# A sixth slot for expert weights in the room of the rotary and retention buffers

## The chip, the core and the metric

One core of a Trainium2 chip runs the whole kernel. TensorE does the matrix products and the transposes, VectorE (DVE), ScalarE (ACT) and GpSimd (POOL) the rest; SyncE (SP) only issues transfers. The metric is the device time of one execution in microseconds.

## The reference, cut to what matters

One layer of a decoder trunk on 512 tokens of width 1024, all in float32: a mixing sub-layer (sparse attention beside retention), then a channel sub-layer, a mixture of experts. What the change touches is the second:

```python
g_prob = softmax(t @ w_group + b_group);  g_top, g_sel = top_k(g_prob, 1)      # 4 groups
e_logits = (t @ w_expert + b_expert) of that group                             # 8 experts each
e_top, e_sel = top_k(softmax(e_logits), 2)
weights = g_top * e_top / sum(e_top)
for e in range(32):
    hid = silu(t @ w_gate_exp[e]) * (t @ w_up_exp[e])                          # 1024 -> 256, twice
    y = y + combine[:, e:e+1] * (hid @ w_down_exp[e])                          # 256 -> 1024
out = h_res + gate2 * rms_norm(y, g_post_ffn)
```

So 512 tokens give 1024 pairs of a token and an expert, and each of the 32 experts has 3 MiB of weights, of which every byte is needed once.

## The kernel before, in words

**Mixing stage.** Projections, rotary embedding, attention and retention run from a list of steps that `Plan` writes out by hand; each engine walks the same list. The rotary products live in `ropebuf` (2048 words of each partition), relu rows, attention transposes and the retention's inner products in `retbuf` (2560), attention masks in `score` (1152), the angles' cosines and sines in `cosT` and `sinT` (256 each), queries, keys and values in `work` (8704). Then come the output projection, the residual and the second norm, whose rows `H2` are stored to DRAM by POOL (L1693) and turned for the router.

**Routing.** `routing` on DVE turns the router's logits into the two experts of each token, counts and ranks the pairs (TensorE sums over partitions, L820 to L823), sorts the experts by count (`KEY`, `BEATS`, `PLACE`) and writes for each row of each unit which pair stands there (`pid_t`) and which token (`tok_t`). Its scratch, some thirty small tensors, lies in `retbuf` and `ropebuf`. The first two units need only the first four experts' ranks and get their rows early (`EARLY_...`, `early_tok`); the others wait for the table (`IN_ROW`, `IN_BOTH`, `late_rows`, `tok_ready`).

**Expert stage.** 32 experts are worked on in 18 units (`UNITS`), in this order: three pairs of the fixed experts 0 to 5, four pairs of less used ones, four units of one much used expert each, and seven pairs. A pair shares the 128 rows, 64 each; a single expert has all 128. `ORDER` is the experts' positions in order of use, 0 to 31, and position n has the weight slot n mod `SLOTS`. Of unit u TensorE does `turn_x` (L873: transposes of the gathered rows), `gate_up` (L883: both products into one bank), `turn_hid` (L901) and `down` (L910), in the order gate_up(u+1), turn_hid(u), turn_x(u+2), down(u). ACT and DVE gate the products, weigh the result by `row_wt` and write it to `YO`; POOL scatters it to DRAM (L1712).

**Weights.** There are five slots of 3 MiB: four in `ring`, which the mixing stage's weights used before, and the fifth over `rows` (gate and up) and the upper half of `hT` (down). `load_gate_up` (L460) issues two transfers of 1 MiB, `load_down` (L467) one, all by SP, in this order: gate and up of slots 0 and 3, the input once more, the downs of 0 and 3 after the retention, slots 1 and 2 after the output projection, slot 4 after the last row of `H2` and the last modulation. Then the refills: for unit u SP waits for gate_up(u) and loads gate and up of the positions that take its slots (`LET_IN`), and then, after down(u-1), the downs of the positions that take the slots of u-1. Names above the fixed six are read from the sorted list (`order_ready`, `value_load`).

```python
LET_IN = {u: [p for p in ORDER[SLOTS:] if UNIT_OF[ORDER[POS[p] - SLOTS]] == u] for u in range(NU)}
```

**Gathers.** POOL brings a unit's rows from DRAM into one of four buffers `XG` of 1024 words in `work`, one after another: gathers 0 and 1 after `early_tok`, 2 and 3 after `tok_ready`, and then, for each u, gather(u+4) and scatter(u). Each waits for the turning of the unit that had its buffer.

**Tail.** When all pairs are scattered, ACT reads them back, DVE adds each token's two, and the last norm and the residual follow (`combine`, `weigh`, `finish`).

Of the kernel before, what the change touches and what calls it, by code (L numbers as in the profile page):

```python
# [42 lines left out]
NOV = 2 * S // HALF  # L43
FIXED, WIDE = 6, 4
SLOTS = 5
FIRST_UNITS = 2
NEARLY = FIRST_UNITS * 2
# [4 lines left out]
NU = len(UNITS)  # L52
# [34 lines left out]
C_ID, C_CAUSAL, C_LT, C_ONES, C_FREQ, C_IOTA = 0, 128, 256, 384, 512, 576  # L87
# [146 lines left out]
def build(nc, t, out):  # L234
    plan = Plan()
    steps = plan.steps

    with ExitStack() as ctx:
        def sb(name, words, dt=F32, parts=P):
            return ctx.enter_context(nc.sbuf_tensor(name, [parts, words], dt))  # L240

        def sem(name):
            return ctx.enter_context(nc.semaphore(name))
# [5 lines left out]
        ring = sb("ring", RING * SLOT)  # L249
        xs = sb("xs", NB * D)  # L250
        hT = sb("hT", KD * S)
        work = sb("work", 4 * 2048 + 512)
        retbuf = sb("retbuf", 2560)
        ropebuf = sb("ropebuf", 2048)
        rows = sb("rows", 4 * D)
        accB, G1, S2, T2 = (rows[:, i * D:(i + 1) * D] for i in range(4))
        score = sb("score", P * (2 + 3 + 4))
        cst = sb("cst", NCONST)
        cosT = sb("cosT", NB * 64)
        sinT = sb("sinT", NB * 64)  # L260
# [12 lines left out]
        ones = cst[:, C_ONES:C_ONES + P]  # L273
# [24 lines left out]
        def gate_and_up(s):  # L298
            return ring[:, s * SLOT:s * SLOT + 2 * KD * F] if s < RING else rows[:, :]

        def down_rows(s):
            return ring[:, s * SLOT + 2 * KD * F:(s + 1) * SLOT] if s < RING else hT[:, KD * S // 2:KD * S // 2 + KF * D]

# [35 lines left out]
        unit_done, tp_done, sc_done, o_done = sem("unit_done"), sem("tp_done"), sem("sc_done"), sem("o_done")  # L339
# [18 lines left out]
        router_done = sem("router_done")  # L358
        xg_in = [sem(f"xg_in{i}") for i in range(RING)]
        gu_in = [sem(f"gu_in{i}") for i in range(SLOTS)]  # L360
# [44 lines left out]
        def bank(use):  # L405
            return ps[plan.bank[use]]
# [42 lines left out]

        XG = [work[:, (4 + i) * D:(5 + i) * D] for i in range(RING)]  # L450
        XT = [hT[:, i * KD * P:(i + 1) * KD * P].rearrange("p (k c) -> p k c", k=KD) for i in range(2)]
# [54 lines left out]
        def rt(at, n):  # L506

            return retbuf[:, at:at + NB * n].rearrange("p (b n) -> p b n", b=NB)
        LG, GMAX, GSUBV, GEXV, GSUM, GTOP = rt(0, 36), rt(144, 1), rt(152, NG), rt(168, NG), rt(184, 1), rt(188, 1)
# [5 lines left out]
        OH1, OH2, RANK = rt(704, NE), rt(832, NE), rt(960, NE)  # L515
        CNT, OV, BINC, BEX = (retbuf[:, 1088:1120], retbuf[:, 1248:1280], retbuf[:, 1280:1312], retbuf[:, 1312:1344])
        MFL, TMP = rt(1120, NE), rt(1600, NE)
        KEY, PLACE, ROOM, FIRST = (retbuf[:, 1472 + i * NE:1472 + (i + 1) * NE] for i in range(4))
        LATE, BIG, SHIFT, ORDV, EXC = (retbuf[:, 2288 + i * NE:2288 + (i + 1) * NE] for i in range(5))
        TILE, ROW = (retbuf[:, at:at + 2 * NB].rearrange("p (b j) -> p b j", b=NB) for at in (1728, 1736))  # L520
        WHERE = retbuf[:, 1744:1744 + 2 * NB].rearrange("p (b j) -> p b j", b=NB)
        OVC = retbuf[:, 1760:1760 + NOV * NE].rearrange("p (o e) -> p o e", o=NOV)
        EO = retbuf[:, 2448:2448 + NOV]
        BEATS = ropebuf[:, 0:NE * NE].rearrange("p (e f) -> p e f", e=NE)

        IN_ROW = ropebuf[:, 0:2 * NB * P].rearrange("p (n c) -> p n c", n=2 * NB)
        IN_BOTH = ropebuf[:, 1024:1024 + 4 * NB * NT].rearrange("p (n w t) -> p n w t", n=2 * NB, w=2)
        IN_TILE, IN_WT = IN_BOTH[:, :, 0, :], IN_BOTH[:, :, 1, :]
        row_wt = retbuf[:, 1408:1408 + NT]

        CUM = retbuf[:, 1344:1472].rearrange("p (b n) -> p b n", b=NB)
        BOTH = retbuf[:, 704:960].rearrange("p (j b e) -> p j b e", j=2, b=NB)
        RANK_AT, EARLY_AT = rt(2464, NEARLY), rt(2480, NEARLY)
        EARLY_MUL = retbuf[:, 2496:2528].rearrange("p (j b e) -> p j b e", j=2, b=NB)
        EARLY_POS, SECOND, EARLY_ROW = (retbuf[:, 2528 + i * 2 * NB:2536 + i * 2 * NB] for i in range(3))
        EARLY_PAIR = retbuf[:, 228:244].rearrange("p (t n) -> p t n", t=2)
        EARLY_IN = ropebuf[:, 1024:2048].rearrange("p (n c) -> p n c", n=2 * NB)
        SORTED, WHOLE = (retbuf[:, 1344 + i * NE:1376 + i * NE] for i in range(2))


        @block.sync
        def _(sp):
# [31 lines left out]
            for e in (0, 3):  # L574
                load_down(sp, e, e, down_in[e])
            for e in (1, 2):
                sp.wait_ge(*used_up(LAST_IN[e]))
                load_gate_up(sp, e, e, gu_in[e])
                load_down(sp, e, e, down_in[e])
            sp.wait_ge(h2_ready, NB)  # L580
            sp.wait_ge(mod_done, 8)
            load_gate_up(sp, RING, RING, gu_in[RING])
            load_down(sp, RING, RING, down_in[RING])
            named = {p: p for p in range(FIXED)}
            for u in range(NU + 1):
# [26 lines left out]
        def _(pe):  # L612
# [149 lines left out]
            def project():  # L762
# [56 lines left out]
                o = take(pe, ("rank",))  # L819
                pe.matmul(o[:, 0:NB * NE], cst[:, C_LT:C_LT + P], retbuf[:, 256:384], start=True, stop=False)  # L820
                pe.wait_ge(oh_ready, 2)
                pe.matmul(o[:, NE:NB * NE], ones, retbuf[:, 1344:1344 + (NB - 1) * NE], start=False, stop=True)
                pe.matmul(o[:, NB * NE:(NB + 1) * NE], ones, CUM[:, NB - 1, :], start=True,  # L823
# [46 lines left out]
            def turn_x(u):  # L870
                pe.wait_ge(xg_in[u % RING], 16 * (u // RING + 1))
                for q in range(2):
                    if u >= 1:  # L873
                        pe.wait_ge(xt_ev, 2 * u - 1 + q)
                    v = XG[u % RING].rearrange("p (q k) -> p k q", k=KD)
                    for c in range(4):
                        mm = pe.transpose(ps[XT_BANK[q]][:, c * P:(c + 1) * P], v[:, 4 * q + c, :], ident)
                    mm.then_inc(xt_mm, 1)
# [286 lines left out]
        def _(dve):  # L1165
# [136 lines left out]
            def routing():  # L1302
# [4 lines left out]
                def flat(x):  # L1307
                    return x.rearrange("p b n -> p (b n)")
# [7 lines left out]

                prod = retbuf[:, 384:512].rearrange("p (b e g) -> p b e g", b=NB, e=EPG)
                for b in range(NB):
                    last = v.tensor_tensor(prod[:, b, :, :], LG[:, b, NG:].rearrange("p (g e) -> p e g", g=NG),
                                           SG[:, b, :].unsqueeze(1).to_broadcast([P, EPG, NG]), ALU.mult)  # L1320
                link(last)
                link(v.tensor_reduce(flat(EL), retbuf[:, 384:512].rearrange("p (q g) -> p q g", g=NG), AX, ALU.add))
                first_best(EL, EMAX, ET, EM, numbers(EPG), EPG, O1)
# [18 lines left out]
                dve.wait_ge(rank_done, 1)  # L1342
                link(v.tensor_copy(retbuf[:, 960:1120], bank(("rank",))[:, 0:(NB + 1) * NE]))
                link(v.tensor_tensor(RANK_AT, RANK[:, :, 0:NEARLY],
# [313 lines left out]
        def _(pool):  # L1658
# [41 lines left out]
            def gather(u):  # L1700

                if u >= RING:
                    pool.wait_ge(xt_mm, 2 * (u - RING) + 2)
                    pool.wait_ge(xg_in[u % RING], 16 * (u // RING))
                g.indirect_dma_start(out=XG[u % RING], out_offset=None, in_=h2_dram,
                                     in_offset=bass.IndirectOffsetOnAxis(ap=tok_t[:, u:u + 1], axis=0),
                                     bounds_check=token_bound, oob_is_err=False).then_inc(xg_in[u % RING], 16)

# [6 lines left out]

            for u in range(RING):
                if u == FIRST_UNITS:
                    pool.wait_ge(tok_ready, 1)
                gather(u)
            for u in range(NU):  # L1720
                if u + RING < NU:
                    gather(u + RING)
                scatter(u)
# [47 lines left out]
```

## Time and profile before

| | |
|---|---|
| median of 3 runs | 743.2 us (742.86 to 745.53) |
| the profiled execution | 741.91 us |
| its span | 739.8 us |
| TensorE, matmuls | 647.3 us busy (88% of the span) |
| TensorE, weight loads | 320.5 us (43%) |
| DVE | 373.4 us (50%) |
| ACT | 159.8 us (22%) |
| POOL | 79.4 us (11%) |
| DMA | 171.76 MB, mean 232 GB/s |
| granted TensorE clock, mean | 0.966 |

The span runs from the first to the last instruction; the execution's own time has 2.1 us more around it. Busy shares are averages over stages with different limits, so the page's 40 slices and the table of stages say more than this one. A busy TensorE is not TensorE at its peak: matmuls are pipelined and their ends are modelled. Idle time of an engine is put down to what ended it, and to "issue" where nothing that the profile follows did, as with a wait for a transfer of SP's queue.

### The profile page before, as it was taken

What the parts mean: (1) busy time and instruction counts of PE and PEld (TensorE: products, weight loads), DVE (VectorE), ACT (ScalarE), POOL (GpSimd) and SP (SyncE); (2) the same over time, 40 slices, a digit from 0 to 9 for tenths busy, and PEclk for the clock granted to TensorE, in tenths of its full rate; (3) what the DMA queues carried; (4) which work ended last, traced back from release to release, by engine and by line L of the source; (5) the groups of instructions that cost most, each with busy time, mean ns of one, the idle gap of its engine ahead of it and who ended that gap; (6) DMA issues with size and microseconds to landing.
All of it is one profiled execution on the core that took longest, in us unless ns stands there. A gap on an engine that the chain in (4) does not pass through costs nothing. (4 is left out here: it accounts for less than half of the span.)

```text
span 739.8 us, 7183 instructions
## 1 busy us (share of the span) xinstructions
PE 647.3 (88%) x2514; PEld 320.5 (43%) x2514; DVE 373.4 (50%) x722; ACT 159.8 (22%) x334; POOL 79.4 (11%) x105
## 2 busy tenths in 40 slices
PE   1699999999999999999999988999788999878730
PEld 1455544444455555556644554433233544333210
DVE  5764266989776763247933258623112233212218
ACT  1420021133122223310222231112111212111113
POOL 0013221210111110000000001121111221200010
PEclk9999999999999999999999999999989999999975
DMA  9991706150606060250641085799999999999426
GB/s 327 389 346 64 277 3 226 23 205 5 224 0 228 2 223 5 106 156 3 262 193 57 29 353 204 292 418 420 422 420 421 421 410 394 420 419 412 163 77 270
DMA packets 50132, 171.76 MB, mean 232 GB/s; under 512 B 10032, under 2 KB 10032, under 8 KB 37168
## 3 DMA queue, kind: packets, MB, share of 16 engines
q1 hardware_dynamic: 41824, 154.98, 53.9%
q0 software_dynamic: 5888, 10.52, 3.8%
q10 hardware_dynamic: 2384, 5.80, 2.1%
q8 instruction: 21, 0.34, 0.2%
q14 instruction: 15, 0.12, 0.0%
HBM read 168.13 MB, written 13.63 MB: 246 GB/s over the span
## 5 line engine op out<-in xcount | busy, mean ns | idle before, releaser
L623 PE MATMUL psum<-ring,hT 128*128 128x512 f32 (+1 forms) x576 | 234.8, 561 | 0.0
L623 PEld LDWEIGHTS psum<-ring,hT 128*128 128x128 f32 x576 | 102.7, 191 | 119.3 <-issue 119.0
L897 PE MATMUL psum<-ring,hT 128*64 128x512 f32 (+1 forms) x416 | 127.8, 635 | 19.5 <-issue 19.5
L897 PEld LDWEIGHTS psum<-ring,hT 128*64 128x64 f32 (+1 forms) x416 | 43.6, 152 | 90.8 <-issue 90.6
L1593 DVE TENSOR_SCALAR work<-work 128x256 f32<-128x256 f32 x18 | 5.3, 294 | 141.2 <-PE psum L907 114.4
L923 PE MATMUL psum<-ring,work 128*64 128x512 f32 (+1 forms) x208 | 63.4, 613 | 5.1 <-issue 3.6
L774 PE MATMUL psum<-ring,hT 128*128 128x512 f32 x128 | 55.8, 594 | 1.6 <-ACT work L1060 0.9
L1207 DVE SCALAR_TENSOR_TENSOR rows<-ring,sm,rows 128x512 f32<-128x512 f32 x64 | 51.1, 799 | 1.7
L897 PE MATMUL psum<-rows,hT 128*64 128x512 f32 (+1 forms) x96 | 42.4, 595 | 1.8 <-issue 1.8
L1105 ACT ACTIVATE work<-psum 128x256 f32<-128x256 f32 x18 | 6.9, 383 | 171.0 <-PE psum L897 171.0
L1268 DVE TENSOR_TENSOR ropebuf<-psum,cosT 128x512 f32<-128x512 f32 (+1 forms) x24 | 14.7, 614 | 51.4 <-PE psum L623 39.1
L1712 POOL DMA_INDIRECT pair_rows<-work,pid_t x18 | 18.0, 1000 | 204.8 <-DVE work L1605 204.8
L1675 POOL TENSOR_TENSOR ropebuf<-ropebuf 128x256 f32<-128x256 f32 (+1 forms) x28 | 18.8, 673 | 180.0 <-DVE ropebuf L1268 180.0
L774 PEld LDWEIGHTS psum<-ring,hT 128*128 128x128 f32 x128 | 24.0, 190 | 30.7 <-issue 29.7
L923 PEld LDWEIGHTS psum<-ring,work 128*64 128x64 f32 (+1 forms) x208 | 20.1, 147 | 31.8 <-issue 30.9
L998 ACT ACTIVATE work<-psum 128x512 f32<-128x512 f32 (+1 forms) x24 | 12.6, 542 | 90.3 <-PE psum L635 85.0
L1595 DVE RECIPROCAL work<-work 128x256 f32<-128x256 f32 x18 | 31.5, 1753 | 0.6
L1605 DVE TENSOR_SCALAR work<-psum,retbuf 128x512 f32<-128x512 f32 x18 | 13.5, 751 | 33.4 <-PE psum L923 33.4
L645 PE MATMUL psum<-cst,work 128*64 128x1 f32 x64 | 8.3, 259 | 23.1 <-DVE work L1207 23.1
L1280 DVE MAX8 sm<-score 128x8 f32<-128x256 f32 (+2 forms) x48 | 26.9, 560 | 1.4
L1489 DVE CUSTOM_DVE_ANT_0 xs<-psum,score 128x256 f32<-128x256 f32 (+2 forms) x24 | 12.4, 555 | 29.4 <-PE psum L727 29.4
L1281 DVE MATCH_REPLACE8 score<-sm,score 128x256 f32<-128x256 f32 (+2 forms) x48 | 26.0, 542 | 0.0
(245 smaller groups left out, 737.7 us busy)
## 6 DMA issues: line engine op xcount, KB each, us to landing
ring<-in_w_gate_exp SPq DMA_DIRECT2D x26, 1024.0 KB, 13.7
ring<-in_w_up_exp SPq DMA_DIRECT2D x26, 1024.0 KB, 21.4
ring<-in_w_down_exp SPq DMA_DIRECT2D x26, 1024.0 KB, 23.1
ring<-in_w_in SPq DMA_DIRECT2D x8, 2048.0 KB, 10.0
ring<-in_w_ada SPq DMA_DIRECT2D x8, 2048.0 KB, 14.9
ring<-in_w_ada SPq DMA_DIRECT2D x7, 1024.0 KB, 13.1
rows<-in_w_gate_exp SPq DMA_DIRECT2D x6, 1024.0 KB, 14.0
rows<-in_w_up_exp SPq DMA_DIRECT2D x6, 1024.0 KB, 22.3
```

Source lines behind the costliest of these rows:

```text
L623: mm = pe.matmul(o[:, 0:width], hT3[:, k, b * P:(b + 1) * P], w[:, k, :], start=(k == 0), stop=(k == KD - 1))
L774: mm = pe.matmul(o[:, :], hT3[:, k, b * P:(b + 1) * P], w[:, k, :], start=(k == 0), stop=(k == KD - 1))
L897: mm = pe.matmul(o[rows, :], XT[u % 2][:, k, rows], both(SLOT_OF[place])[:, k, :, :], start=(k == 0), stop=(k == KD - 1))
L923: mm = pe.matmul(o[rows, :], HT[u % 2][:, i, rows], down_of(SLOT_OF[place])[:, i, n * 512:(n + 1) * 512], start=(i == 0), stop=(i == KF - 1))
L1207: ins = v.scalar_tensor_tensor(out=acc, in0=w[:, k, :], scalar=sc_[:, k:k + 1], in1=acc, op0=ALU.mult, op1=ALU.add)
L1268: ins = v.tensor_tensor(dst, src, tb, ALU.mult)
L1280: link(v.max(top8, m))
L1281: link(v.match_replace(m, top8, m, TAKEN))
L1595: v.reciprocal(e, e).then_inc(gu_step, 1)
L1605: v.tensor_scalar(YO[u % 2][:, 512:1024], ps[Y_BANK[(2 * u + 1) % 3]][:, :], row_wt[:, u:u + 1], None, ALU.mult).then_inc(y_evV, 1)
L1675: g.tensor_tensor(dst[:, :, 0, :], xc[:, :, 0, :], xs_[:, :, 1, :], ALU.subtract)
L1712: g.indirect_dma_start(out=y_dram, out_offset=bass.IndirectOffsetOnAxis(ap=pid_t[:, u:u + 1], axis=0), in_=YO[u % 2], in_offset=None, boun ...
```

## The change

The number of slots goes from 5 to 6. The new slot's gate and up lie over `ropebuf` and the first 2048 words of `retbuf`, which become one tensor, `both_bufs`; its down lies over words 6144 to 8191 of `work`, where `H2[1]`, an ACT scratch and the gather buffers 2 and 3 were. The gathers keep two buffers. What the routing kept in the two old buffers goes to `score`, `cosT`, `sinT`, the lower 2048 words of `work` and the last 512 words of `retbuf`. The order of the refills follows from `SLOTS`. POOL issues gathers 0, 1 and 2 at the start and then, for each u, gather(u+3) and scatter(u).

```diff
-SLOTS = 5
+SLOTS = 6
+GATHERS = 2
...
-        retbuf = sb("retbuf", 2560)
-        ropebuf = sb("ropebuf", 2048)
+        both_bufs = sb("both_bufs", 2048 + 2560)
+        ropebuf, retbuf = both_bufs[:, 0:2048], both_bufs[:, 2048:4608]
...
         def gate_and_up(s):
-            return ring[:, s * SLOT:s * SLOT + 2 * KD * F] if s < RING else rows[:, :]
+            if s < RING:
+                return ring[:, s * SLOT:s * SLOT + 2 * KD * F]
+            return rows[:, :] if s == RING else both_bufs[:, 0:2 * KD * F]
 
         def down_rows(s):
-            return ring[:, s * SLOT + 2 * KD * F:(s + 1) * SLOT] if s < RING else hT[:, KD * S // 2:KD * S // 2 + KF * D]
+            if s < RING:
+                return ring[:, s * SLOT + 2 * KD * F:(s + 1) * SLOT]
+            return hT[:, KD * S // 2:KD * S // 2 + KF * D] if s == RING else work[:, 6 * D:8 * D]
...
-        xg_in = [sem(f"xg_in{i}") for i in range(RING)]
+        xg_in = [sem(f"xg_in{i}") for i in range(GATHERS)]
...
-        XG = [work[:, (4 + i) * D:(5 + i) * D] for i in range(RING)]
+        XG = [work[:, (4 + i) * D:(5 + i) * D] for i in range(GATHERS)]
...
-            return retbuf[:, at:at + NB * n].rearrange("p (b n) -> p b n", b=NB)
+            return score[:, at:at + NB * n].rearrange("p (b n) -> p b n", b=NB)
...
-        BEATS = ropebuf[:, 0:NE * NE].rearrange("p (e f) -> p e f", e=NE)
-
-        IN_ROW = ropebuf[:, 0:2 * NB * P].rearrange("p (n c) -> p n c", n=2 * NB)
+        BEATS = work[:, 0:NE * NE].rearrange("p (e f) -> p e f", e=NE)
+
+        IN_ROW = work[:, 0:2 * NB * P].rearrange("p (n c) -> p n c", n=2 * NB)
...
@@ SP @@
             for e in (0, 3):
                 load_down(sp, e, e, down_in[e])
+            sp.wait_ge(ret_ss, RHEADS)
+            load_gate_up(sp, RING + 1, RING + 1, gu_in[RING + 1])
             for e in (1, 2):
...
             load_down(sp, RING, RING, down_in[RING])
+            sp.wait_ge(h2_out[1], 16 * (NB // 2))
+            sp.wait_ge(res_sq, NB)
+            sp.wait_ge(tp_done, plan.tp[("h2", NB - 1, 1)] + 1)
+            load_down(sp, RING + 1, RING + 1, down_in[RING + 1])
...
@@ TensorE @@
-                pe.wait_ge(xg_in[u % RING], 16 * (u // RING + 1))
+                pe.wait_ge(xg_in[u % GATHERS], 16 * (u // GATHERS + 1))
...
@@ POOL @@
-                if u >= RING:
-                    pool.wait_ge(xt_mm, 2 * (u - RING) + 2)
-                    pool.wait_ge(xg_in[u % RING], 16 * (u // RING))
+                if u >= GATHERS:
+                    pool.wait_ge(xt_mm, 2 * (u - GATHERS) + 2)
+                    pool.wait_ge(xg_in[u % GATHERS], 16 * (u // GATHERS))
...
-            for u in range(RING):
+            for u in range(GATHERS + 1):
                 if u == FIRST_UNITS:
                     pool.wait_ge(tok_ready, 1)
                 gather(u)
             for u in range(NU):
-                if u + RING < NU:
-                    gather(u + RING)
+                if u + GATHERS + 1 < NU:
+                    gather(u + GATHERS + 1)
                 scatter(u)
```

## Rows read from the trace of the kernel before

**Rows 1.** The page, 40 slices of 18.5 us: TensorE and DMA busy tenths, transfer rate.

```profile
PE   1699999999999999999999988999788999878730
...
DMA  9991706150606060250641085799999999999426
GB/s 327 389 346 64 277 3 226 23 205 5 224 0 228 2 223 5 106 156 3 262 193 57 29 353 204 292 418 420 422 420 421 421 410 394 420 419 412 163 77 270
```

**Rows 2.** Stage table: us, engines' busy us, last three: granted clock, DMA share, GB/s.

```profile
452.80:466.50 13.70, 12.41 (x57) 5.30 (x56) 12.16 (x56) 2.18 (x5) 2.09 (x2) 1.00 0.09 24
522.40:574.40 52.00, 44.49 (x165) 17.98 (x166) 10.94 (x15) 7.78 (x15) 5.04 (x5) 0.88 1.02 421
574.40:621.70 47.30, 47.30 (x166) 21.72 (x166) 14.59 (x20) 10.19 (x20) 9.07 (x9) 1.00 0.99 407
666.40:691.90 25.50, 20.19 (x102) 8.30 (x99) 7.29 (x10) 5.26 (x10) 1.98 (x2) 1.00 0.91 373
```

**Rows 3.** Instructions in order of time, TensorE: start, us, line; bracket: idle before.

```profile
456.80 1.16 PE L877 MATMUL psum<-cst,work 128*128 128x128 f32 x8 [0.95 <-DMA work<-h_rows,tok_t]
...
459.36 7.09 PE L897 MATMUL psum<-ring,hT 128*64 128x512 f32 x32
...
522.37 8.43 PE L897 MATMUL psum<-ring,hT 128*64 128x512 f32 x32 [5.11 <-issue]
...
605.97 0.64 PE L897 MATMUL psum<-ring,hT 128*64 128x512 f32 x1
...
613.33 1.06 PE L877 MATMUL psum<-cst,work 128*128 128x128 f32 x8
...
617.75 7.09 PE L897 MATMUL psum<-ring,hT 128*64 128x512 f32 x32
...
691.87 8.78 PE L897 MATMUL psum<-ring,hT 128*64 128x512 f32 x32 [3.45 <-issue]
...
706.53 3.65 PE L923 MATMUL psum<-ring,work 128*64 128x512 f32 x16 [0.68 <-ACT work L1111]
```

**Rows 4.** Issues of SP's queue in order of time: start, us that the issue took.

```profile
372.51 0.81 SPq L469 DMA_DIRECT2D ring<-in_w_down_exp  x2
...
466.49 0.33 SPq L464 DMA_DIRECT2D ring<-in_w_gate_exp  x1
...
652.07 0.33 SPq L464 DMA_DIRECT2D rows<-in_w_gate_exp  x1
...
670.23 0.38 SPq L465 DMA_DIRECT2D ring<-in_w_up_exp  x1
...
675.02 13.77 SPq L469 DMA_DIRECT2D ring<-in_w_down_exp  x2
```

**Rows 5.** Issue to landing of the last up half, issued at 670.23 (L465).

```profile
DMA to landing us min/median/max: 21.5/21.5/21.5
```

**Rows 6.** DMA queues, 675 to 695 us in 40 parts of 0.5 us: rate.

```profile
GB/s 442 426 442 410 393 426 426 442 426 410 434 352 443 377 475 336 402 311 344 279 295 295 279 229 246 197 229 229 197 213 262 377 426 459 393 238 107 131 98 98
```

**Rows 7.** Issue to landing of the last down half, issued at 688.5 (L469).

```profile
DMA to landing us min/median/max: 11.4/11.4/11.4
```

**Rows 8.** Issue to landing of the first refill's gate half, 466.49 (L464).

```profile
DMA to landing us min/median/max: 4.9/4.9/4.9
```

**Rows 9.** Instructions in order of time, POOL: store of h2, gathers (L1705).

```profile
435.09 0.53 POOL L1693 DMA_DIRECT2D h_rows<-work  x1 [15.87 <-DVE work L1581]
453.47 1.07 POOL L1705 DMA_INDIRECT work<-h_rows,tok_t  x1 [17.86 <-issue]
...
597.50 1.01 POOL L1705 DMA_INDIRECT work<-h_rows,tok_t  x1 [0.30 <-issue]
```

**Rows 10.** Issue to landing of h2's last store, issued at 435.09 (L1693).

```profile
DMA to landing us min/median/max: 8.6/8.6/8.6
```

**Rows 11.** Issue to landing of slot 4's first down, issued at 435.66 (L469).

```profile
DMA to landing us min/median/max: 17.0/17.0/17.0
```

**Rows 12.** Issue to landing of all 18 gathers (L1705).

```profile
DMA to landing us min/median/max: 3.3/10.1/12.7
```

More of the change, by code:

```diff
@@ L506, in rt, with spare @@
         def rt(at, n):
-            return retbuf[:, at:at + NB * n].rearrange("p (b n) -> p b n", b=NB)
+            return score[:, at:at + NB * n].rearrange("p (b n) -> p b n", b=NB)
+        def spare(at, n):
+            return retbuf[:, 2048 + at:2048 + at + n]
         LG, GMAX, GSUBV, GEXV, GSUM, GTOP = rt(0, 36), rt(144, 1), rt(152, NG), rt(168, NG), rt(184, 1), rt(188, 1)
@@ L515, in build @@
         OH1, OH2, RANK = rt(704, NE), rt(832, NE), rt(960, NE)
[L516 to L520, printed above, removed]
@@ L521, in build @@
-        WHERE = retbuf[:, 1744:1744 + 2 * NB].rearrange("p (b j) -> p b j", b=NB)
-        OVC = retbuf[:, 1760:1760 + NOV * NE].rearrange("p (o e) -> p o e", o=NOV)
-        EO = retbuf[:, 2448:2448 + NOV]
-        BEATS = ropebuf[:, 0:NE * NE].rearrange("p (e f) -> p e f", e=NE)
-        IN_ROW = ropebuf[:, 0:2 * NB * P].rearrange("p (n c) -> p n c", n=2 * NB)
-        IN_BOTH = ropebuf[:, 1024:1024 + 4 * NB * NT].rearrange("p (n w t) -> p n w t", n=2 * NB, w=2)
-        IN_TILE, IN_WT = IN_BOTH[:, :, 0, :], IN_BOTH[:, :, 1, :]
@@ L529, in build @@
[L529 to L536, printed above, removed]
@@ L537, in build @@
-        EARLY_IN = ropebuf[:, 1024:2048].rearrange("p (n c) -> p n c", n=2 * NB)
-        SORTED, WHOLE = (retbuf[:, 1344 + i * NE:1376 + i * NE] for i in range(2))
+        CNT = score[:, 1088:1120]
+        MFL, TMP = (cosT[:, i * P:(i + 1) * P].rearrange("p (b n) -> p b n", b=NB) for i in range(2))
+        KEY, PLACE, ROOM, FIRST = (sinT[:, i * NE:(i + 1) * NE] for i in range(4))
+        LATE, BIG, SHIFT, ORDV, EXC, OV, BINC, BEX = (spare(i * NE, NE) for i in range(8))
+        TILE, ROW, WHERE = (spare(256 + i * 2 * NB, 2 * NB).rearrange("p (b j) -> p b j", b=NB) for i in range(3))
@@ new lines, in build @@
+        EARLY_POS, SECOND, EARLY_ROW = (spare(280 + i * 2 * NB, 2 * NB) for i in range(3))
+        EO = spare(304, NOV)
+        OVC = score[:, 384:384 + NOV * NE].rearrange("p (o e) -> p o e", o=NOV)
+        BEATS = work[:, 0:NE * NE].rearrange("p (e f) -> p e f", e=NE)
+        IN_ROW = work[:, 0:2 * NB * P].rearrange("p (n c) -> p n c", n=2 * NB)
+        IN_BOTH = work[:, 1024:1024 + 4 * NB * NT].rearrange("p (n w t) -> p n w t", n=2 * NB, w=2)
+        IN_TILE, IN_WT = IN_BOTH[:, :, 0, :], IN_BOTH[:, :, 1, :]
@@ new lines, in build @@
+        row_wt = sinT[:, 192:192 + NT]
+        CUM = sinT[:, 128:256].rearrange("p (b n) -> p b n", b=NB)
+        BOTH = score[:, 704:960].rearrange("p (j b e) -> p j b e", j=2, b=NB)
+        RANK_AT, EARLY_AT = (spare(at, NB * NEARLY).rearrange("p (b n) -> p b n", b=NB) for at in (320, 336))
+        EARLY_MUL = spare(352, 2 * NB * NEARLY).rearrange("p (j b e) -> p j b e", j=2, b=NB)
+        EARLY_PAIR = score[:, 228:244].rearrange("p (t n) -> p t n", t=2)
+        EARLY_IN = work[:, 1024:2048].rearrange("p (n c) -> p n c", n=2 * NB)
@@ L541, in _ @@
+        SORTED, WHOLE = (sinT[:, 128 + i * NE:128 + (i + 1) * NE] for i in range(2))
         @block.sync
@@ L819, in project @@
                 o = take(pe, ("rank",))
-                pe.matmul(o[:, 0:NB * NE], cst[:, C_LT:C_LT + P], retbuf[:, 256:384], start=True, stop=False)
+                pe.matmul(o[:, 0:NB * NE], cst[:, C_LT:C_LT + P], score[:, 256:384], start=True, stop=False)
                 pe.wait_ge(oh_ready, 2)
-                pe.matmul(o[:, NE:NB * NE], ones, retbuf[:, 1344:1344 + (NB - 1) * NE], start=False, stop=True)
+                pe.matmul(o[:, NE:NB * NE], ones, sinT[:, 128:128 + (NB - 1) * NE], start=False, stop=True)
                 pe.matmul(o[:, NB * NE:(NB + 1) * NE], ones, CUM[:, NB - 1, :], start=True,
@@ L874, in turn_x @@
                         pe.wait_ge(xt_ev, 2 * u - 1 + q)
-                    v = XG[u % RING].rearrange("p (q k) -> p k q", k=KD)
+                    v = XG[u % GATHERS].rearrange("p (q k) -> p k q", k=KD)
                     for c in range(4):
@@ L1315, in routing @@
                 v.tensor_tensor(GSUBV, LG[:, :, 0:NG], GMAX.to_broadcast([P, NB, NG]), ALU.subtract).then_inc(g_sub, 1)
-                prod = retbuf[:, 384:512].rearrange("p (b e g) -> p b e g", b=NB, e=EPG)
+                prod = score[:, 384:512].rearrange("p (b e g) -> p b e g", b=NB, e=EPG)
                 for b in range(NB):
@@ L1321, in routing @@
                 link(last)
-                link(v.tensor_reduce(flat(EL), retbuf[:, 384:512].rearrange("p (q g) -> p q g", g=NG), AX, ALU.add))
+                link(v.tensor_reduce(flat(EL), score[:, 384:512].rearrange("p (q g) -> p q g", g=NG), AX, ALU.add))
                 first_best(EL, EMAX, ET, EM, numbers(EPG), EPG, O1)
@@ L1342, in routing @@
                 dve.wait_ge(rank_done, 1)
-                link(v.tensor_copy(retbuf[:, 960:1120], bank(("rank",))[:, 0:(NB + 1) * NE]))
+                link(v.tensor_copy(score[:, 960:1120], bank(("rank",))[:, 0:(NB + 1) * NE]))
                 link(v.tensor_tensor(RANK_AT, RANK[:, :, 0:NEARLY],
@@ L1700, in gather @@
             def gather(u):
-                if u >= RING:
-                    pool.wait_ge(xt_mm, 2 * (u - RING) + 2)
-                    pool.wait_ge(xg_in[u % RING], 16 * (u // RING))
-                g.indirect_dma_start(out=XG[u % RING], out_offset=None, in_=h2_dram,
+                if u >= GATHERS:
+                    pool.wait_ge(xt_mm, 2 * (u - GATHERS) + 2)
+                    pool.wait_ge(xg_in[u % GATHERS], 16 * (u // GATHERS))
+                g.indirect_dma_start(out=XG[u % GATHERS], out_offset=None, in_=h2_dram,
                                      in_offset=bass.IndirectOffsetOnAxis(ap=tok_t[:, u:u + 1], axis=0),
-                                     bounds_check=token_bound, oob_is_err=False).then_inc(xg_in[u % RING], 16)
+                                     bounds_check=token_bound, oob_is_err=False).then_inc(xg_in[u % GATHERS], 16)
             def scatter(u):
```

## The prediction

> **What bounds the kernel now.** I read the 40 slices first. Up to about 460 us TensorE is the full engine and the DMA engines come and go; from 481 to 684 us the DMA share is 9 tenths or more in every slice and the rate stands at 394 to 422 GB/s [rows 1]. That is the expert stage: 32 experts of three 1 MiB transfers (gate, up, down; 1.049 MB each). The stage table agrees: share 1.02 and 0.99, 421 and 407 GB/s [rows 2]. TensorE looks busy there too, but its own rows show that it waits: gate_up(5) starts at 522.37 after an idle of 5.11 us and gate_up(17) at 691.87 after 3.45 us, both put down to "issue", that is, to nothing that the program's engines did [rows 3]. For the last one the landing can be matched: the up half of the last expert, issued at 670.23, landed 21.5 us later, at 691.7 [rows 4, 5]. So the stage ends when the weights have come, and then 18.3 us of TensorE (to 710.2, the end of down(17)) and 29.6 us of scatter, read-back and output follow.
>
> TensorE's own pace is faster. From gate_up(11) to gate_up(12) it needs 617.75 - 605.97 = 11.8 us without a wait [rows 3]. From gate_up(0) at 459.36, 17 steps of 11.8 us would start gate_up(17) at 660, not 691.9. TensorE therefore has about 32 us of room before it becomes the bound.
>
> **Where the stream of weights starts and what it carries.** The DMA engines are nearly idle from 452.8 to 466.5 us (share 0.09) [rows 2]: all five slots are full, and the next load waits for gate_up(0). It is issued at 466.49 [rows 4]. From there to the landing at 691.7, which are counted in transfers: with five slots 27 experts are still to come, 81 transfers, of which three (the downs of the experts at positions 29, 30 and 31 in order of use) are issued behind the last up: 78. So one transfer costs 225.2 / 78 = 2.89 us, gathers and scatters included. By the mean rate of 421 GB/s it would be 1.049 / 0.421 = 2.49 us. The two differ because a transfer ends when its last DMA engine ends. From 675 to 695 us the rate sinks from 442 to 197 GB/s while the last up is still on its way [rows 6]: most engines are through, some lag. The last down alone, issued at 688.5 into engines that were by then mostly free, took 11.4 us, the first one of the stream, at 466.49, took 4.9 [rows 7, 8].
>
> I take **2.8 us**, near the counted price, since the lagging engines are the ones that end the last up, and keep 2.49 and 2.89 as the ends. The Trainium skill (DMA: Bandwidth & Descriptors, Where 436 GB/s comes from) says that between HBM and SBUF a core's HBM share of about 358 GB/s is what binds; the trace shows 421, so that figure does not hold here. By it a transfer would cost an estimated 2.9 us and four of them 11.7.
>
> **The change, part by part.**
>
> 1. *Sixth slot, count.* 26 experts instead of 27 have to come after gate_up(0): three transfers fewer in the stream.
>
> 2. *Sixth slot, order at the end.* With five slots position 31 reuses the slot of position 26 and is asked for after gate_up(15). With six, positions 30 and 31 follow 24 and 25, both after gate_up(14), where SP now asks for 29 and 30 (the block that starts at 652.07 [rows 4]). The downs of 28 to 31 all stand behind the last up: 78 - 74 = 4 transfers fewer ahead of it, three from point 1 and one from the order. The gain at gate_up(17) is 4 x 2.8 = **11.2 us** (10.0 to 11.6); if the order gave nothing, 3 x 2.49 = 7.5.
>
> 3. *Is the last down in time?* It lands at 688.5 + 11.4 = 699.9 now [rows 7], and three transfers earlier, at about 691.5, after. down(17) would start at 706.53 - 11.2 = 695.3: 3.8 us of cover. If it is gone, its excess is lost one for one.
>
> 4. *Loading the sixth slot.* The gate and up halves are issued behind the downs of slots 0 and 3 (372.51 [rows 4]) and the wait in front of them, for the retention's sums, has ended by then, since the wait before it needs those sums. 2.1 MB go into three slices, 370 to 425 us, with 193, 57 and 29 GB/s [rows 1]: 5 us of DMA, cost nothing. Behind them on SP stand the loads of slots 1 and 2, which wait for the output projection and start after those slices, so SP loses two issues in an idle time. Without that cover the price would be 5 us.
>
> 5. *The down half of the sixth slot.* It waits for the last store of h2: issued at 435.09, landed after 8.6 us, so at 443.7 [rows 9, 10]. Then it queues behind slot 4, whose down was issued at 435.7 and landed 17.0 us later, at 452.7 [rows 11], and ends at about 455.2. The first gather is issued at 453.47 and TensorE waited 0.95 us for it at 456.80 [rows 9, 3]. It now runs beside the end of that load. Nothing to 2.5 us; I take **+0.5 us**, since most of the transfer lies ahead of the gather. The wait on SP costs nothing: the refill behind it is due at 466.49.
>
> 6. *The refill.* The first two are now positions 6 and 7, and both names come from the sorted list on SP; reading the first stands ahead of the wait for gate_up(0). No cost.
>
> 7. *Two gather buffers.* After scatter(u-1) POOL issues gather(u+3) instead of gather(u+4). In the tightest stretch the issue is at 597.50, and as it would be gather(12), it is due at turn_x(12), 613.33 [rows 9, 3]: 15.8 us, against 10.1 median and 12.7 longest [rows 12]. The wait for the turning of unit u+1 has ended by then, and scatter(u) behind it is not held up. Cost nothing, with 3.1 us of cover; beyond, each excess delays a unit.
>
> 8. *The routing's scratch.* Same instructions and shapes, other addresses, no new wait; BEATS and IN_ROW lie in rooms that the same engine has finished with, and YO is written after the table. No cost; I put 0.5 us either way in the range.
>
> Sum: -11.2 + 0.5 = -10.7 us. The profiled execution took 741.9 us (span 739.8); the median of the runs is 743.2, 1.3 above. So 731.2 for such an execution and **732.5 us** for the median. TensorE stays off the bound: gate_up(17) at 681, against the 660 that it could reach.
>
> **Rivals.**
>
> *A. Only the count helps (12%).* If the lagging engines do not set the end, or the order gives nothing, 3 x 2.49 = 7.5 us less 1 to 3 of points 5 and 3: 737 to 739. For it: the mean rate is nearly flat; against: the matched landing.
>
> *B. The slots also starved the stream (14%).* The share is 0.99 and 407 GB/s in the stretch of single experts and 0.91 and 373 at the end [rows 2]. Full rate would give back 47.3 x 14/421 = 1.6 us and 25.5 x 48/421 = 2.9 us: -15.2, or 728.
>
> *C. The gathers become the bound (slower, 4%).* With two buffers a gather that lands more than 15.8 us after its issue stops TensorE in every unit. The loop then runs over two units, so an excess counts once in two. To be slower by 3.7 us gate_up(17) must start at 695.6, 35.6 us behind TensorE's own 660; over the 14 units from the fourth on, seven loops, that is 5.1 us each, a landing time of 20.9 us. At 22 us it is 7 x 6.2 = 43 us, gate_up(17) at 703.4, 11.5 later than now: 755. Against it: the landing time does not follow the depth of the weight queue. Its longest was 12.7 us, while the last up took 21.5 from issue to landing [rows 12, 5]. The Trainium skill (DMA: Bandwidth & Descriptors, Queues, rings and completion order) has each DMA engine go round between its queues packet by packet, so a longer weight queue would not push a gather back; the trace agrees.
>
> *D. No difference (7%).* The stream itself gets slower, because it is deeper. With 74 transfers a price of 3.03 us instead of 2.89 gives the whole gain back: 743, between 740 and 746. For it: the counted price is above the mean already, so the DMA engines are not evenly loaded; against: the rate was level from 481 to 592 us [rows 1]. TensorE's clock decides nothing here: it was granted 0.88 from 522.4 to 574.4, where TensorE waited for weights, and 1.00 behind that [rows 2], and gate_up took 8.43 us rather than 7.09 [rows 3], but such a loss lies inside time that the weights set. At the last unit (8.78 us) it is in the 18.3 us already.
>
> The main case keeps 63%. Its own range is 730 to 735. A gain below 0.5% (3.7 us) could not be told from none. The range reaches to B at the lower end and to A at the upper: 727.5 to 738.5. Faster by over 0.5%: main, A and B, 0.89; same 0.07; slower 0.04.
>
> **What would show it.** Right: no wait before gate_up(5); gate_up(17) starts near 681, still after a wait, with the last up landing just before; DMA share near 1 up to about 680; 29.6 us after down(17) as before; gathers land in 10 to 13 us and no turn_x from the third on waits for one. Point 2 is wrong if the gain at gate_up(17) is near 7.5 while three transfers fewer are gone; point 5 if gate_up(0) starts after 460.4. The whole is wrong if gate_up(17) starts without a wait for weights, or if TensorE waits for gathers in the middle of the stage.

## The result and the profile after

| | before | after |
|---|---|---|
| median | 743.03 us (4 runs, 741.62 to 745.53) | 730.72 us (4 runs, 730.48 to 731.33) |
| ratio | | 0.9833, interval 0.9812 to 0.9853 |
| profiled execution, its span | 741.91 us, 739.8 us | 730.83 us, 728.6 us |

12.3 us less by the medians, 11.1 by the profiled executions. The forecast was 732.5 us with a range of 727.5 to 738.5. A second set of runs of the same kernel (e5 below) had 733.9 us beside 743.9 for the kernel before, 10.0 us less: the forecast lies between the two sets.

The page's slices of the kernel after, for [rows 1]:

```profile
PE   1599999999999999999999989999997999788830
...
PEclk9999999999999999999999999999998999999975
DMA  9991806060705042070391059399999999999526
GB/s 327 391 359 34 299 15 231 0 231 0 232 0 197 34 130 103 2 237 29 130 396 81 30 233 400 127 415 421 421 418 423 420 419 421 420 417 413 220 89 264
```

The rate now stands between 413 and 423 GB/s from the 27th slice to the 37th; the dip to 394 of the 34th slice before (610 to 629 us, right behind the units of single experts) is gone. A table of stages shows the stretch of those units (last three columns: granted clock, DMA share, GB/s), and how the last gate_up was clocked:

```profile
570.00:620.00 50.00, 48.41 (x181) 21.54 (x179) 16.05 (x23) 11.07 (x21) 8.07 (x8) 1.00 1.02 420
682.70:689.70 7.00, 7.00 (x33) 2.59 (x33) 0.00 (x0) 0.00 (x0) 0.80 (x1) 1.00 0.38 155
```

TensorE in order of time, for [rows 3]; the bracket is the idle time ahead:

```profile
457.49 1.16 PE L892 MATMUL psum<-cst,work 128*128 128x128 f32 x8 [1.16 <-DMA work<-h_rows,tok_t]
...
460.04 7.09 PE L912 MATMUL psum<-ring,hT 128*64 128x512 f32 x32
...
607.02 1.51 PE L912 MATMUL psum<-ring,hT 128*64 128x512 f32 x6 [0.61 <-issue]
...
682.66 7.09 PE L912 MATMUL psum<-ring,hT 128*64 128x512 f32 x32 [1.74 <-issue]
...
695.62 3.65 PE L938 MATMUL psum<-ring,work 128*64 128x512 f32 x16 [0.68 <-ACT work L1126]
```

gate_up(0) starts at 460.04, gate_up(17) at 682.66, 222.6 us later. Before it was 691.87 - 459.36 = 232.5 [rows 3]. **That distance is the measure of all that follows**, since it leaves out how the mixing stage went. The difference is 9.9 us. gate_up(5) no longer waits; the first wait for weights comes in unit 6, ahead of down(6). Behind gate_up(17) stand 16.6 us to the end of down(17) at 699.27, against 18.3 before, and 29.3 against 29.6 to the end of the span. So the span's 11.2 us are 9.9 at the last weights, 1.7 in the last gate_up (7.09 against 8.78 us), 0.3 in the tail, less 0.7 by which gate_up(0) starts later.

SP's issues, for [rows 4]: the down of the sixth slot, the first refill, the last up half, the last two downs.

```profile
444.37 0.33 SPq L474 DMA_DIRECT2D work<-in_w_down_exp  x1
467.33 0.36 SPq L469 DMA_DIRECT2D ring<-in_w_gate_exp  x1
...
654.98 2.14 SPq L470 DMA_DIRECT2D ring<-in_w_up_exp  x1
...
663.62 5.35 SPq L474 DMA_DIRECT2D ring<-in_w_down_exp  x2
```

From issue to landing, of the last up half (L470):

```profile
DMA to landing us min/median/max: 27.6/27.6/27.6
```

It landed at 682.6, and gate_up(17) started at 682.66: the stage still ends with the weights. The gathers (L1720), for [rows 12]:

```profile
DMA to landing us min/median/max: 3.5/10.2/11.9
```

### The profile page after: what moved, and what is told of

It reads as the page before. It is cut to its first block and busy times, and to the rows that moved or that the text cites. A ratio compares the mean times of both kernels' runs of the same rounds, so it can differ in the third digit from the quotient of the medians.

```text
span 728.6 us, 7186 instructions
## 1 busy us (share of the span) xinstructions
PE 644.6 (88%) x2514; PEld 319.8 (44%) x2514; DVE 373.5 (51%) x722; ACT 159.8 (22%) x334; POOL 79.5 (11%) x105
## 5 line engine op out<-in xcount | busy, mean ns | idle before, releaser
L912 PE MATMUL psum<-ring,hT 128*64 128x512 f32 (+1 forms) x352 | 85.0, 594 | 4.4 <-issue 4.4
L912 PEld LDWEIGHTS psum<-ring,hT 128*64 128x64 f32 (+1 forms) x352 | 30.0, 142 | 57.2 <-issue 56.2
L938 PE MATMUL psum<-ring,work 128*64 128x512 f32 (+1 forms) x176 | 46.5, 632 | 4.7 <-issue 4.1
L912 PE MATMUL psum<-rows,hT 128*64 128x512 f32 (+1 forms) x80 | 38.6, 639 | 8.4 <-issue 8.4
L1283 DVE TENSOR_TENSOR both_bufs<-psum,cosT 128x512 f32<-128x512 f32 (+1 forms) x24 | 14.7, 614 | 51.4 <-PE psum L638 39.1
L912 PE MATMUL psum<-both_bufs,hT 128*64 128x512 f32 (+1 forms) x80 | 38.6, 640 | 0.0
L1690 POOL TENSOR_TENSOR both_bufs<-both_bufs 128x256 f32<-128x256 f32 (+1 forms) x28 | 18.8, 673 | 180.4 <-DVE both_bufs L1283 180.4
L1013 ACT ACTIVATE work<-psum 128x512 f32<-128x512 f32 (+1 forms) x24 | 12.6, 542 | 90.3 <-PE psum L650 85.0
L1620 DVE TENSOR_SCALAR work<-psum,sinT 128x512 f32<-128x512 f32 x18 | 13.5, 751 | 34.9 <-PE psum L938 34.9
L912 PEld LDWEIGHTS psum<-rows,hT 128*64 128x64 f32 (+1 forms) x80 | 12.4, 157 | 32.6 <-issue 32.6
```

The source lines that it names most:

```text
L912: mm = pe.matmul(o[rows, :], XT[u % 2][:, k, rows], both(SLOT_OF[place])[:, k, :, :], start=(k == 0), stop=(k == KD - 1))
L938: mm = pe.matmul(o[rows, :], HT[u % 2][:, i, rows], down_of(SLOT_OF[place])[:, i, n * 512:(n + 1) * 512], start=(i == 0), stop=(i == KF - 1))
L1013: a.activation(dst, src, ACT.Copy).then_inc(evac, 1)
L1283: ins = v.tensor_tensor(dst, src, tb, ALU.mult)
L1620: v.tensor_scalar(YO[u % 2][:, 512:1024], ps[Y_BANK[(2 * u + 1) % 3]][:, :], row_wt[:, u:u + 1], None, ALU.mult).then_inc(y_evV, 1)
L1690: g.tensor_tensor(dst[:, :, 0, :], xc[:, :, 0, :], xs_[:, :, 1, :], ALU.subtract)
```

## The experiments

Nine more kernels ran and the changed one once more (e5), each timed beside the kernel before on the same chip; the ratio is to that one, whose median was 743.1 to 743.9 us in these sets. In the table "distance" is that from gate_up(0) to gate_up(17), in the profiled execution.

| kernel | median, us | ratio to before (interval) | distance, us | last gate_up, us |
|---|---|---|---|---|
| before | 743.0 | | 232.5 | 8.78 |
| after | 730.7 | 0.983 (0.981 to 0.985) | 222.6 | 7.09 |
| e1 | 740.8 | 0.996 (0.993 to 0.999) | 230.1 | 8.78 |
| e2 | 743.8 | 1.000 (0.998 to 1.001) | 232.5 | 8.69 |
| e3 | 739.0 | 0.993 (0.991 to 0.994) | 227.9 | 9.19 |
| e4 | 732.6 | 0.984 (0.982 to 0.986) | 221.0 | 7.09 |
| e5 (after again) | 733.9 | 0.986 (0.982 to 0.989) | 222.5 | 8.78 |
| e6 | 727.3 | 0.978 (0.975 to 0.980) | 218.4 | 7.09 |
| e7 | 730.0 | 0.981 (0.979 to 0.984) | 216.7 | 8.74 |
| e8 | 731.5 | 0.983 (0.980 to 0.987) | 221.4 | 7.09 |
| e9 | 731.0 | 0.982 (0.978 to 0.986) | 221.3 | 7.09 |
| e10 | 737.4 | 0.991 (0.988 to 0.995) | 228.3 | 8.78 |

### e1: the sixth slot filled late

```diff
-            sp.wait_ge(ret_ss, RHEADS)
-            load_gate_up(sp, RING + 1, RING + 1, gu_in[RING + 1])
...
+            sp.wait_ge(gu_mm, 1)
+            load_gate_up(sp, RING + 1, RING + 1, gu_in[RING + 1])
             load_down(sp, RING + 1, RING + 1, down_in[RING + 1])
```

> The changed kernel with six slots, but the sixth slot's three transfers are asked for only after gate_up(0), at the head of the refills. Theory (the gain is the number of transfers that stand between gate_up(0) and the last up half, 2.9 us each): 77 of them stand there instead of 74 in the changed kernel and 78 in the one before, so gate_up(17) starts about 8.7 us later than in the changed kernel and the time is 739 to 741 us. Rival (six slots help because the stream is starved less with five, whenever the sixth is filled): most of the gain stays, 731 to 734 us.

740.8 us, as the theory expected (739 to 741); gate_up(0) and gate_up(17):

```profile
461.73 7.09 PE L912 MATMUL psum<-ring,hT 128*64 128x512 f32 x32
...
691.79 8.78 PE L912 MATMUL psum<-ring,hT 128*64 128x512 f32 x32 [2.09 <-issue]
```

The theory holds: six slots without the early fill keep only 2.4 of the 9.9 us. The price is smaller than expected, though: 7.5 us for three transfers, 2.5 each and not 2.9.

### e2: two gather buffers and five slots

The edit is that of the change to `XG`, `xg_in`, `gather` and the two loops that call it, on the kernel before.

> The kernel before with five slots and two gather buffers instead of four, nothing else. Theory (a gather lands within 13 us and has 15.8): no difference, 742 to 744 us, and no turning of rows waits for a gather from unit 3 on. Rival (the second half of the buffers was worth something and the changed kernel pays for it): slower by 1 us or more, with waits for gathers in the stretch of single experts.

743.8 us, distance 232.5. What TensorE waited for from 470 to 700 us (us in total, times, longest):

```profile
PE psum L898 <- issue: 19.7, 7, 3.8
PE psum L924 <- issue: 6.3, 2, 5.5
PE psum L878 <- DMA work<-h_rows,tok_t: 1.4, 1, 1.4
```

One wait for a gather, the one of unit 2 behind the table, which the kernels before and after have too. The two buffers cost nothing.

### e3: the last expert's gate and up behind two downs

```diff
+            held = []
             for u in range(NU + 1):
                 for place in LET_IN.get(u, []):
+                    if place == ORDER[-1]:
+                        named[place] = ...
+                        held.append(place)
+                        continue
...
                     load_down(sp, named[place], SLOT_OF[place], down_in[SLOT_OF[place]])
+                if held:
+                    place = held.pop()
+                    load_gate_up(sp, named[place], SLOT_OF[place], gu_in[SLOT_OF[place]])
```

> The changed kernel, but gate and up of the last expert (position 31) are issued behind the downs of positions 28 and 29 instead of ahead of them: 76 transfers instead of 74 up to the last up half. Theory (each transfer ahead of the last up costs 2.5 to 2.9 us at the end, whichever it is): 735.7 to 736.5 us, gate_up(17) later by 5 to 6 us. Rival (only the number of experts that come after gate_up(0) counts, the order at the end gives nothing): 730 to 731.5 us.

739.0 us, more than either expected. gate_up(0) and gate_up(17):

```profile
460.85 7.09 PE L921 MATMUL psum<-ring,hT 128*64 128x512 f32 x32
...
688.72 9.19 PE L921 MATMUL psum<-ring,hT 128*64 128x512 f32 x32 [7.03 <-issue]
```

The distance grew by 5.3 us, 2.6 for each of the two transfers: the order at the end counts as much as the number. SP's issue of the last up half came at 660.19 instead of 654.98 us and its landing 6.0 us later: with the order the issue moved as well. The rest of the 8.3 us between the profiled spans (736.9 and 728.6) is the clock of the last gate_up, 2.1 us longer behind a wait of 7.03 us, and a start 0.8 us later.

### e4 and e5: the first refill in halves, and the changed kernel again

```diff
+            for piece in range(PIECES):
+                sp.wait_ge(*((gu_piece, piece + 1) if piece < PIECES - 1 else (gu_mm, 1)))
+                for place in LET_IN[0]:
+                    slot, w = SLOT_OF[place], KD * F
+                    at, lo, hi = gate_and_up(slot), piece * w // PIECES, (piece + 1) * w // PIECES
+                    sp.dma_start(at[:, lo:hi], pick(wg_d, named[place])[:, lo:hi]).then_inc(gu_in[slot], 16)
+                    sp.dma_start(at[:, w + lo:w + hi], pick(wu_d, named[place])[:, lo:hi]).then_inc(gu_in[slot], 16)
...
+                    if u == 0 and k < KD - 1 and (k + 1) % (KD // PIECES) == 0:
+                        mm.then_inc(gu_piece, 1)
```

> The changed kernel, but gate and up of the first two refills (positions 6 and 7) are loaded in two halves each: the halves that gate_up(0) has read by its middle are asked for there, 3.5 us before its end. Theory (the stream of weights is the bound from its first transfer to its last up half, so what starts it earlier ends it earlier): 3 to 3.5 us less, 727 to 728 us. Rival (the start of the stream does not set its end, since somewhere between the engines wait for free slots): 730 to 731.5 us.

> The changed kernel as it is, as the level for the two kernels beside it. From gate_up(0) to gate_up(17) it should need 222 to 223 us as in its first profile, and 730 to 732 us in all. If the halved first refill had really cost time in the run before (732.6 us), this one must come out below it by over 1 us relative to the kernel before; if that was the start of the run alone, the two are equal in relation to it.

732.6 us, where the changed kernel had 730.7 in one set of runs and 733.9 in another. gate_up(0) and (17) of e4, then of e5:

```profile
464.10 7.09 PE L925 MATMUL psum<-ring,hT 128*64 128x512 f32 x32
...
685.12 7.09 PE L925 MATMUL psum<-ring,hT 128*64 128x512 f32 x32 [1.76 <-issue]
```

```profile
463.33 7.09 PE L912 MATMUL psum<-ring,hT 128*64 128x512 f32 x32
...
685.86 8.78 PE L912 MATMUL psum<-ring,hT 128*64 128x512 f32 x32 [2.08 <-issue]
```

The distance of e5 is 222.5 us, as in the first profile, but its gate_up(0) came at 463.33 and its last gate_up took 8.78 us: the same code is 5.1 us longer in this execution (733.7 against 728.6), all of it outside the distance. Of the 3.3 us by which gate_up(0) came later, 2.5 arose between the last store of `H2` (435.55 and 436.06) and the first gather (453.96 and 457.00), and there TensorE's clock did it. Here are the router's last-but-one products (L811), the modulation's (L700) and the stretch from 432 to 436 us (third number from the right: granted clock), first in the changed kernel and then in e5:

```profile
430.16 1.98 PE L811 MATMUL psum<-work 128*128 128x36 f32 x16 [0.79 <-ACT work L1013]
431.97 1.96 PE L700 MATMUL psum<-rows,cst 128*128 128x512 f32 x4
...
432.00:436.00 4.00, 3.48 (x14) 1.70 (x14) 3.42 (x5) 0.44 (x3) 0.45 (x1) 1.00 1.01 420
```

```profile
430.67 3.51 PE L811 MATMUL psum<-work 128*128 128x36 f32 x16 [0.79 <-ACT work L1013]
433.99 3.76 PE L700 MATMUL psum<-rows,cst 128*128 128x512 f32 x4
...
432.00:436.00 4.00, 4.00 (x14) 2.97 (x14) 2.67 (x3) 0.95 (x3) 0.00 (x0) 0.50 1.01 426
```

From that store to the first gather it is 20.9 us in e4, e5, e6 and e7, 19.3 in e1 and 18.4 in all others. The changed kernel itself had a granted clock of 0.50 from 440 to 442 us, where only TensorE's filling products were running and it cost nothing. The three traces with five slots have no such loss there; the same code has it or not (e5 and the changed kernel), so whether six slots make it more frequent is open. By the distance, which leaves this out, the halves are a gain of 1.5 us, not the 3.5 by which their stream starts earlier, and nothing that the medians show; e5's own median, 733.9, lies above the 730 to 732 that it was expected to have. So neither the theory nor its rival holds as put: something under half arrives. Where the rest goes was not settled.

### e6, e7 and e10: the rows of a unit spread over the partitions

```diff
+    c[:, C_SPREAD + r // HALF * HALF + r % HALF // 32 * 32 + r % 8 * 4 + r // 8 % 4] = r + 1
...
-                v.tensor_tensor(IN_ROW, in_pairs(ROW, P), iota(P), ALU.is_equal)
+                v.tensor_tensor(IN_ROW, in_pairs(ROW, P), cst[:, C_SPREAD:C_SPREAD + P].unsqueeze(1).to_broadcast(
+                    [P, 2 * NB, P]), ALU.is_equal)
```

`EARLY_IN` compares with the same constants, and the row numbers start at 1.

> The changed kernel, but the rows of a unit lie in another order within each half of 64 partitions: row r at partition 32*(r/32) + 4*(r mod 8) + (r/8 mod 4), so that 8 neighbouring rows lie 4 partitions apart. Gathers and scatters leave empty rows out, and the full ones stand at the start of each half, so the DMA engines that serve those partitions move more. Theory (this load is what makes some DMA engines lag, and the lag, not the mean rate, ends the last up half): the lag of up to 20 us between first and last engine of one transfer shrinks, gate_up(17) comes 6 to 9 us earlier and the time is 722 to 725 us. Rival (certain DMA engines are slow whatever rows they move): 730 to 732 us and the rate sinks before the last landing as before.

> The spread rows together with the first refill in halves (asked for 3.5 us earlier). Theory (one stream from its start to its last landing, and without the lag nothing else holds it up): 2.5 to 3.5 us less than with the spread rows alone. Rival (the earlier start is lost again within the stage): less than 1 us of difference to the spread rows alone.

> The kernel before, five slots and four gather buffers, with the spread rows alone. Theory (a part of its 232.5 us from gate_up(0) to gate_up(17) is the lag of the DMA engines that move the full rows, the same with five slots as with six, and no part of the price of a transfer): 3.5 to 4.5 us less there, 738 to 740 us. Rival (the lag builds up only with the deeper queue of six slots, or the spread rows help by something else): no difference to the kernel before, 742 to 744 us.

e6: 727.3 us, the fastest of the study; its interval lies wholly below that of e5, timed beside it. Expected were 722 to 725 us and 6 to 9 us in the stage, so the theory has the direction and too large a size. gate_up(0) and (17) of e6:

```profile
463.00 7.09 PE L915 MATMUL psum<-ring,hT 128*64 128x512 f32 x32
...
681.42 7.09 PE L915 MATMUL psum<-ring,hT 128*64 128x512 f32 x32 [1.71 <-issue]
```

The distance fell by 4.1 us. How the lag went shows in the rate, in 40 parts of 0.625 us. The changed kernel, 660 to 685 us:

```profile
GB/s 420 420 419 419 419 393 419 433 419 419 419 419 419 419 406 374 446 400 393 420 393 380 367 380 367 393 341 354 301 301 301 288 288 288 288 249 236 236 236 203
```

The same stretch with the rows spread:

```profile
GB/s 407 419 419 406 419 433 419 419 419 419 419 419 419 439 406 439 393 407 406 433 433 433 419 419 419 419 433 406 433 433 419 406 393 380 341 315 354 308 236 210
```

In the first the rate is below 400 GB/s for nearly all of the last 12 us, in the second for the last 5: the DMA engines finish closer together. (gate_up(17) starts at 682.66 us in the first and at 681.42 in the second.) The traces hold the same more directly, in the times of a transfer's sixteen semaphore increments, taken here for the ends of sixteen engines' shares: those of the last down half run from 673.2 to 693.1 us in the changed kernel, 19.9 us, and from 680.2 to 691.7 in e6, 11.5 us. With five slots, for the down half of position 30, it is 14.3 us in the kernel before and 8.9 in e10. Nothing but the rows' places differs, so how the rows lie sets a good part of the lag. That the full rows side by side at the start of each half load some engines more is the reading that the order was made for; no view shows which engines they are.

The Trainium skill (DMA: Bandwidth & Descriptors, The descriptor swizzle) says for a transfer over 128 partitions which of them one engine serves, four neighbours and the four that lie 32 above. The order of e6 was made after it, and the run agrees in so far as spreading by it helped; the section does not speak of gathers of single rows. The Trainium skill (DMA: Bandwidth & Descriptors, Latency and other measured facts) names two engines as usually slower than the others. No run here shows that, but something of the kind may be what is left: the rate still sinks at the end.

The same edit on the kernel before (e10) gave 737.4 us and a distance of 228.3, 4.2 less. The lag is there with five slots as with six and has no share in the change. With the halves as well (e7) the distance is 1.7 us shorter still, nearly as between e5 and e4 (1.5), but the last gate_up took 8.74 us instead of 7.09 and the median is 2.7 us above that of e6. Neither side of its expectation came: the theory wanted 2.5 to 3.5 us less, the rival under 1 us of difference. The median's loss is not explained by the two traces, whose spans are 727.6 and 727.3 us; e6's is that of its slowest execution.

### e8 and e9: dummy products ahead of the last gate_up

e8 is e6 with this edit, e9 is e7 with it.

```diff
+                if u == NU - 1:
+                    pe.wait_ge(xt_ev, 2 * NU)
+                    stream(ps[XT_BANK[0]], 4)
```

> The changed kernel with spread rows, and before gate_up(17) TensorE runs four dummy products into a free bank (1.7 us) where it used to wait for the last weights. Theory (the longer last gate_up, 8.8 instead of 7.1 us in some executions, comes from the idle wait ahead of it): gate_up(17) takes 7.1 us, its start is not later, and the median is 0 to 1.7 us below the spread rows alone (726 to 727.5 us). Rival (the clock answers to the longer waits of the units before, or to nothing that TensorE does here): 8.8 us again in about half of the executions, the time as with the spread rows alone.

> Spread rows, the first refill in halves and the dummy products together. From gate_up(0) to gate_up(17) 216.7 us as with the first two; with the last gate_up at 7.1 instead of 8.7 us the time is 724 to 726 us if the theory of the clock holds, 727 to 730 us if it does not.

A miss, by a size: the four products of e8 took 3.70 us, not 1.7.

```profile
679.35 3.70 PE L778 MATMUL psum<-cst 128*128 128x512 f32 x8
682.98 7.09 PE L918 MATMUL psum<-ring,hT 128*64 128x512 f32 x32
```

gate_up(17) ran at 7.09 us in both, but 3 us (e8) and 4.6 us (e9) later than without them by the distance, and the medians, 731.5 and 731.0, are above those of e6 and e7 and above all that was expected of either. The theory of the clock is neither shown nor refuted by them: the wait and the clock were changed with a delay that hides the gain. It stands on the other rows: after waits of 1.71 to 1.76 us the last gate_up took 7.09 us (after, e4, e6), after waits of 2.08 to 3.47 it took 8.69 to 8.78 (before, e1, e2, e5, e7, e10), after 7.03 it took 9.19. The length of the wait alone does not decide, though: earlier gate_ups took 7.09 us after 2.07 us in the changed kernel and after 2.25 in e4, where e5's last one took 8.78 after 2.08.

```profile
654.11 7.09 PE L925 MATMUL psum<-ring,hT 128*64 128x512 f32 x32 [2.25 <-issue]
```

In the table of stages, the stretch of e5's last gate_up has a granted clock of 0.80:

```profile
685.90:694.60 8.70, 8.70 (x33) 3.13 (x33) 0.00 (x0) 0.00 (x0) 0.46 (x1) 0.80 0.33 138
```

## Why the prediction was right, point by point

**The bound.** Right. The stage ended with the last up half before and after, TensorE started gate_up(17) within 0.1 us of its landing, and moving transfers ahead of it or behind it moved the end (e1, e3).

**The price of a transfer** is the term that was mis-sized. The prediction took 2.8 us, near the 2.89 that it had counted, "since the lagging engines are the ones that end the last up". Measured as a difference it is 9.9 / 4 = 2.5 us in the change, 2.5 in e1 and 2.6 in e3, the mean rate's 2.49, its lower end. The count of 225.2 us over 78 transfers had put into the price what does not go with their number. Of the 225.2 us 78 x 2.49 = 194 are weights. The row of the software queue in the changed kernel, from 460 to 740 us, is the next part (packets, MB, share):

```profile
q0 software_dynamic: 4896, 8.08, 7.6%
```

8.08 MB at 421 GB/s are at most 19 us of gathers and scatters, the same with any number of slots. The 12 us that are left are put down to the lag and the latency, and 4.1 to 4.2 of them went away with the spread rows, with five slots and with six. So the lag was rightly seen and wrongly charged: a lag that every run has falls out of a difference.

**The order at the end** (point 2) was right: e3 has 2.6 us for each transfer put ahead, so rival A, in which it gives nothing, is out. In the change it is one transfer of four, 2.5 us.

**The last down** (point 3) kept 2.6 of the 3.8 us of cover. It landed 29.0 us after its issue at 664.05, at 693.05, and down(17) started at 695.62.

**Filling the sixth slot** (points 4 and 5). Gate and up hid as forecast: POOL's issues ran 0.45 us behind those of the kernel before at 114 us, long ahead of that load, and 0.46 behind at the last store of `H2`, behind it. The down was issued at 444.37 and landed 12.6 us later, beside the first gather; TensorE waited 1.16 us for that instead of 0.95. 0.2 us, where 0.5 was put; the other 0.5 us of gate_up(0)'s later start came with POOL's issue at 453.96 instead of 453.47 and so from what was there at 114 us already. e5 shows that gate_up(0) can differ by 3 us between executions of one kernel, mostly by TensorE's clock.

**The gathers** (point 7). Right: 10.2 us median and 11.9 longest beside a deeper queue of weights, no wait from unit 3 on, and e2 alone 0.9995 of before. Rival C needed more than 15.8 us and did not come.

**Rival B** was half true and gave nothing. The stream did run a little below its rate there (407 GB/s from 574.4 to 621.7 us [rows 2]), and with six slots it runs at 420 GB/s. But e1, which has the six slots and hardly the gain, and a distance that shrank by four times 2.5 us leave no room for it. A likely reason, not tried by itself, is that the engines that ran dry were the early ones, and the late ones set the landing. **Rival D** did not come either: the stream was no slower for being deeper.

**What made up for it.** The sum was 10.7 us and the profiled execution 11.1, because the last gate_up ran in 7.09 us. The prediction took its 8.78 us as part of a fixed 18.3; it goes with TensorE's clock behind the last wait, and e5 had it back. So the number is in part luck: the price was 1.3 us too high over four transfers, and the clock gave 1.7 us that no term of the sum had. -9.9 with the runs' own spread around it is the change's part, and the last 1.7 us come and go.

## What to carry to other kernels

Where a stage runs at the pace of one stream of transfers, a slot is worth what it takes out of the stream between its start and the landing that ends it: count the transfers ahead of that landing, before and after, and price the difference at the mean rate, not at elapsed time over count, which holds everything that stays. Filling the slot while the engines are idle is the gain; the slot itself, filled late, gave a quarter of it. And look at where the full rows of a gather lie: leaving empty rows out saves bytes, but here, with the full rows side by side, the stream ended 4.1 us later than with them spread.

## What the runs showed of the hardware that was not expected

Where gathers and scatters skip rows, other places for the full rows took 4.1 us (six slots) and 4.2 us (five slots) off a stream of 220 to 230 us, and 0.9% off the time of the kernel before (e10); the sixteen increments of the last down half then spread over 11.5 us instead of 19.9. The same program's gate_up(0) came at 460.04 us in one execution and at 463.33 in another, and 2.5 us of that are a stretch ahead of the routing in which TensorE was granted half its clock, 1.2 of 2.4 GHz (0.50 from 432 to 436 us). TensorE's granted clock was 0.80 over the 8.70 us of the last gate_up after a wait of 2.08 us for weights, and 1.00 after 1.74 us; but after a wait of 2.25 us gate_up took 7.09 us as well.
